# One 3 MB load in place of two for the first expert of each late pair, in a mixture-of-experts kernel

## What is computed

```python
routed = moe_dispatch(x, eidx, gates, lw['exp_w_gate'], lw['exp_w_up'], lw['exp_w_down'])
shared = swiglu(x, lw['sh_w_gate'], lw['sh_w_up'], lw['sh_w_down'])
# swiglu: (silu(x @ w_gate) * (x @ w_up)) @ w_down
```

## Time and profile before

| | us |
|---|---|
| median of 3 runs | 1326.27 |
| lowest and highest | 1323.79, 1328.75 |
| the profiled execution | 1324.62 |
| its span, first to last instruction | 1322.5 |
| TensorE busy in it | 1224.0 |
| ScalarE, VectorE busy | 239.2, 280.4 |

### The profile page before, as it was taken

One profiled execution on the slowest core, in us unless ns is written; L12 is line 12 of the kernel. 1 busy time (PEld: TensorE's weight loads), 2 busy tenths in 40 slices (PEclk: granted clock), 3 DMA queues, 4 the chain that ended last, 5 costly groups with the idle time before them and its releaser, 6 DMA issues.

```text
span 1322.5 us, 22616 instructions
## 1 busy us (share of the span) xinstructions
PE 1224.0 (93%) x9596; PEld 836.7 (63%) x9596; DVE 280.4 (21%) x720; ACT 239.2 (18%) x533; POOL 2.8 (0%) x13
## 2 busy tenths in 40 slices
PE   7999999998998898889989999999899898889896
PEld 4566687666766465556565658866667564557464
DVE  1252362110011010111034425511010110011012
ACT  2363131110010110011034521411010101010102
POOL 0000000000000000000000000000000000000000
PEclk9999999999999898889999999999999998899899
DMA  9879849999999999999956653999999999999993
GB/s 401 329 311 352 348 183 420 401 424 408 428 425 426 424 428 427 427 424 424 422 238 252 248 230 146 418 415 424 426 408 421 425 429 425 426 425 429 423 420 160
DMA packets 51796, 496.60 MB, mean 375 GB/s; under 512 B 8848, under 2 KB 9104, under 8 KB 10256
## 3 DMA queue, kind: packets, MB, share of 16 engines
q1 hardware_dynamic: 47664, 493.62, 89.8%
q10 hardware_dynamic: 4064, 2.00, 0.5%
HBM read 493.60 MB, written 2.00 MB: 375 GB/s over the span
## 4 chain that ended last, share of the span: by engine, by line
PE 54%; DMA 36%; SPq 3%; DVE 3%; issue 2%; ACT 1%; DVEq 0%; ACTq 0%
DMA gu<-in_exp_w_both 33%; PE PS L2214 17%; PE PS L1718 7%; PE PS L2050 4%; PE PS L2141 4%; PE PS L2250 4%; PE PS L2148 3%; PE PS L1660 2%; DMA xh<-in_exp_w_both 2%; PE PS L1628 1%; PE PS L2099 1%; DMA gu<-in_w_in_wide 1%; SPq L621 1%; PE PS L1841 1%; PE PS L1852 1%
## 5 line engine op out<-in xcount | busy, mean ns | idle before, releaser
L2214 PE MATMUL PS<-gu,arena 128*32 128x256 f32 (+1 forms) x2848 | 241.2, 422 | 58.6 <-DMA gu<-in_exp_w_both 58.6
L2214 PEld LDWEIGHTS PS<-gu,arena 128*32 128x32 f32 (+1 forms) x2848 | 133.3, 125 | 154.4 <-DMA gu<-in_exp_w_both 65.8
L2141 PE MATMUL PS<-arena 128*128 128x128 f32 x1408 | 176.3, 278 | 0.5 <-ACT arena L1050 0.5
L2141 PEld LDWEIGHTS PS<-arena 128*128 128x128 f32 x1408 | 164.0, 192 | 17.8 <-issue 16.7
L2214 PE MATMUL PS<-arena 128*64 128x256 f32 x704 | 160.2, 386 | 9.3 <-DMA gu<-in_exp_w_both 9.0
L2148 PE MATMUL PS<-arena 128*128 128x256 f32 x704 | 160.2, 380 | 1.4 <-ACT arena L1033 1.4
L2250 PE MATMUL PS<-dn,arena 128*32 128x512 f32 (+1 forms) x688 | 160.2, 596 | 0.0
L2250 PE MATMUL PS<-arena 128*64 128x512 f32 (+1 forms) x336 | 152.6, 597 | 3.0 <-DVE arena L1533 1.6
L2148 PEld LDWEIGHTS PS<-arena 128*128 128x128 f32 x704 | 130.2, 190 | 20.5 <-ACT arena L1033 3.2
L2214 PEld LDWEIGHTS PS<-arena 128*64 128x64 f32 x704 | 96.1, 139 | 67.5 <-issue 22.8
L1539 DVE TENSOR_TENSOR arena<-arena,PS 128x256 f32<-128x256 f32 x44 | 18.5, 421 | 552.7 <-ACT arena L1046 552.7
(11 more groups left out here) (264 smaller groups left out, 1023.3 us busy)
## 6 DMA issues: line engine op xcount, KB each, us to landing
gu<-in_exp_w_both SPq DMA_DIRECT2D x72, 2048.0 KB, 20.2
dn<-in_exp_w_down SPq DMA_DIRECT2D x86, 1024.0 KB, 25.7
arena<-in_exp_w_down SPq DMA_DIRECT2D x42, 1024.0 KB, 26.4
gu<-in_w_ada_pieces SPq DMA_DIRECT2D x20, 2048.0 KB, 9.1
arena<-in_exp_w_both SPq DMA_DIRECT2D x20, 2048.0 KB, 23.1
gu<-in_exp_w_both SPq DMA_DIRECT2D x34, 1024.0 KB, 19.4
xh<-in_exp_w_both SPq DMA_DIRECT2D x12, 2048.0 KB, 35.4
gu<-in_w_in_wide SPq DMA_DIRECT2D x8, 2048.0 KB, 14.4
```

The lines of the kernel that those rows point to most:

```text
L2141: ins = mmul(PS[:, 4, (c % 4) * P:(c % 4) * P + P], h_tok[:, g, c], onehot[b][:, g], start=(g == 0), stop=(g == 1))
L2214: ins = mmul(PS[w * h:w * h + w, 5, FF * half:FF * half + FF], xg[:, k, w * h:w * h + w], weights[half][:, k], start=(k == 0), stop=(k == ...
```

## The change

The three matrices of an expert are laid side by side per partition: one tensor `in_exp_w` with 24 KB a partition, 3 MB an expert. All expert loads read from it. A gate-and-up load now takes 16 KB of each 24 KB, a down 8 KB, a half 8 KB. In `arena`, `fifth` and `fifth_dn` become neighbours, `fifth_whole`. For m = 3 to 7 the pair's first expert comes as one load of 3 MB, issued where its down was issued, and the sixth's gate and up go ahead of it. It is counted in `pair_in`; `pair_dn_in` then counts only the sixth's down, whose target is adapted in `pair`. TensorE's loop begins one turn later, and turn 3 is written out.

```diff
-        fifth = carve(2 * NC_ * FF)
+        fifth_whole = carve(2 * NC_ * FF + 2 * D)
+        fifth = fifth_whole[:, 0:2 * NC_ * FF]
...
-        fifth_dn = carve(2 * D).rearrange("p (j n) -> p j n", j=2)
+        fifth_dn = fifth_whole[:, 2 * NC_ * FF:].rearrange("p (j n) -> p j n", j=2)
...
+            def expert(l, x):
+                return t["exp_w"][l, bass.ds(x, 1)].rearrange("e p n -> (e p) n")
+
             def gate_and_up(l, x):
-                return t["exp_w_both"][l, bass.ds(x, 1)].rearrange("e p n -> (e p) n")
+                return expert(l, x)[:, 0:2 * BLOCK]
...
             def down(l, x):
-                return t["exp_w_down"][l, bass.ds(x, 1)].rearrange("e (p j) n -> (e p) (j n)", j=2)
+                return expert(l, x)[:, 2 * BLOCK:]
...
+            def load_whole_fifth(l, x, told):
+
+                sp.dma_start(fifth_whole, expert(l, x)).then_inc(S[told], 16)
...
                     sp.wait_ge(S["up_done"], m * 2 + (r0 + 4))
-                    both(range(RING, RING + 2), xp, "pair_in", "pair_up_in")
-                    sp.wait_ge(S["down_done"], m * 2 + (r0 + 4))
-                    for j in range(2):
-                        load_dn(RING + j, l, xp[j], "pair_dn_in")
+                    if last:
+                        both(range(RING, RING + 2), xp, "pair_in", "pair_up_in")
+                        sp.wait_ge(S["down_done"], m * 2 + (r0 + 4))
+                        load_dn(RING, l, xp[0], "pair_dn_in")
+                    else:
+                        load(RING + 1, l, xp[1], "pair_in")
+                        sp.wait_ge(S["down_done"], m * 2 + (r0 + 4))
+                        load_whole_fifth(l, xp[0], "pair_in")
+                    load_dn(RING + 1, l, xp[1], "pair_dn_in")
...
-                def pair(m, early=None, last=False, between=None):
+                def pair(m, early=None, last=False, between=None, whole=False):
...
+                    if last:
+                        dns_in = (S["pair_dn_in"], pair_dns_in + (32 * TURNS - 16 * WHOLE))
+                    elif whole:
+                        dns_in = (S["pair_dn_in"], m * 16 + (16 * (DOWN_TURN + 3) + pair_dns_in))
+                    else:
+                        dns_in = (S["pair_dn_in"], m * 32 + (32 + pair_dns_in))
...
-                with pe.Fori(DOWN_TURN + 1, TURNS - 1) as m:
+                quad(DOWN_TURN + 1)
+                pair(DOWN_TURN + 1)
+                with pe.Fori(DOWN_TURN + 2, TURNS - 1) as m:
                     quad(m)
-                    pair(m)
+                    pair(m, whole=True)
```

More of the change, by code:

```diff
@@ L580, in over_loads @@
                     x = expert_in(sp, l, bass.ds(e, 1))
[L581 to L585, removed]
+                    w = t["exp_w"][l, bass.ds(x, 1)].rearrange("e p n -> (e p) n")
+                    sp.dma_start(gu[:, expert_slot[l][1], :], w[:, 0:2 * NC_ * FF]).then_inc(o["w"], 16)
+                    sp.dma_start(dn[:, 1].rearrange("p j n -> p (j n)"), w[:, 2 * NC_ * FF:]).then_inc(o["w"], 16)
                 sp.wait_ge(o["pe"], E * PE_STEPS * OW + BEFORE)
@@ L596, in _ @@
             BLOCK = NC_ * FF
+            def expert(l, x):
+                return t["exp_w"][l, bass.ds(x, 1)].rearrange("e p n -> (e p) n")
             def gate_and_up(l, x):
-                return t["exp_w_both"][l, bass.ds(x, 1)].rearrange("e p n -> (e p) n")
+                return expert(l, x)[:, 0:2 * BLOCK]
             def gate_or_up(l, x, half):
-                return t["exp_w_both"][l, bass.ds(x, 1), :, half * BLOCK:(half + 1) * BLOCK].rearrange("e p n -> (e p) n")
+                return expert(l, x)[:, half * BLOCK:(half + 1) * BLOCK]
             def down(l, x):
-                return t["exp_w_down"][l, bass.ds(x, 1)].rearrange("e (p j) n -> (e p) (j n)", j=2)
+                return expert(l, x)[:, 2 * BLOCK:]
             def place(j, l):
@@ L2266, in _ @@
                 pairs_in, pair_ups_in = l * 32 * TURNS, l * 32
+                WHOLE = TURNS - 3 - DOWN_TURN
+                pair_dns_in = l * (32 * TURNS - 16 * WHOLE)
                 def quad(m, early=None, last=False):
@@ L2274, in quad @@
                                  (S["quad_dn_in"], m * 64 + 64 * t0))
-                def pair(m, early=None, last=False, between=None):
+                def pair(m, early=None, last=False, between=None, whole=False):
                     second, second_dn = (halves(sixth), dn[:, RING - 1]) if early is None else (own[0], dn[:, 0])
                     ups = [(S["pair_up_in"], pair_ups_in + 32)] if last else []
+                    if last:
[4 more added lines that the diff above has]
+                        dns_in = (S["pair_dn_in"], m * 32 + (32 + pair_dns_in))
                     expert_round(m, 3, (halves(fifth), second), (fifth_dn, second_dn), [(S["pair_in"], m * 32 + (32 + pairs_in))],
-                                 ups, (S["pair_dn_in"], m * 32 + 32 * t0), last=last, between=between)
+                                 ups, dns_in, last=last, between=between)
                 for m in range(DOWN_TURN + 1):
@@ L2373, in laid_out @@
     named["w_ada_first"] = first_third.transpose(2, 0, 1, 3).reshape(NC_ // 2, D, 4 * P)
-    named["exp_w_both"] = np.concatenate([named.pop(n).reshape(DEPTH, E, P, NC_ * FF) for n in ("exp_w_gate", "exp_w_up")],
-                                         axis=-1)
+    named["exp_w"] = np.concatenate([named.pop(f"exp_w_{n}").reshape(DEPTH, E, P, NC_ * FF) for n in ("gate", "up", "down")],
+                                    axis=-1)
     uq = i["mla_w_uq"].reshape(DEPTH, Q_LORA, MLA_H, MLA_QK)
```

## The result

The changed kernel takes 1335.17 us (median of 4 runs, 1334.61 to 1338.0) against 1326.36 us: a ratio of 1.0069, 95% interval 1.0054 to 1.0083. The forecast was 1323.9 us. The profiled execution took 1334.69 us with a span of 1332.6, so 10.1 us more than the span before.

A forecast was written before the change was run, and what follows sets the result against it. The expert load stream at 426 GB/s was taken as the bound. Layer-end gains of 2.0 + 0.4 = 2.4 us took the profiled 1324.62 to 1322.2 us; the median's 1.65 us offset gave 1323.9, range 1319 to 1330.

The forecast's parts named there:

- part 6: TensorE's loop: turn 3 written out gives PE two more rounds as straight code; taken as 0 us.
- Part 1: Pair loads of turns 3 to 7: one load instead of two saves 0.09 us each, 0.9 us in all.
- Part 2: All expert loads: stepping 24 KB between partitions costs 0; bad end, 420 instead of 426 GB/s.
- Part 3: Load stream: the fifth's 2 MB issued 11.2 us later; the stream stays full and the next quad's loads land as before.
- Part 4: Loop pairs: start 1.9 us later in layer 0, 1.4 in layer 1, covered by the quad's wait; price 0.
- Part 5: Layer ends: layer 0's last quad all but loses its pause, gaining 2.0 us; layer 1 gains 0.4 us.
- the pair's wait lengthens the turns: Rival at the pair's first matmul: lateness above 5.1 us slows the turns, 1335 us if 6.0 us late; chance 0.02.
- the 24 KB stride slows the stream: Rival on expert loads: the stream falls to 420 GB/s, 13.5 us more, 1339 us; chance 0.07.
- gap between loads: Rival in the load stream: each load less returns a hidden fixed cost, say 1 us, giving 1316 us; chance 0.04.
- fixed 2 us per load: Rival's larger form in the load stream: ten loads less save 20 us, giving 1306 us.

The follow-up runs named there:

- e2: The kernel before with only turn 3 written out on TensorE, old layout and load order kept: 1336.59 us, ratio 1.0072.
- e1: The changed kernel with turn 3 put back in TensorE's loop instead of written out: 1323.03 us, ratio 0.9975.
- e4: The changed kernel with turn 3 in the loop and the fifth's late load split into 2 and 1 MB: 1326.32 us, ratio 0.9987.
- e3: The kernel before with only the joint layout, all expert loads strided at 24 KB a partition: 1324.63 us, ratio 0.9984.
- e5: The kernel before with 56 matmuls that never run added to each layer's skipped overflow branch: 1338.42 us, ratio 1.0096.

## Why the prediction was wrong

The step that failed is part 6: "PE gets two more rounds as straight code, turns 0 to 2 are so already. [...] I take 0; no row prices it." Its price was 10 us (e2: 1336.59 against 1326.82). The two rounds themselves do run as fast as in the loop: from its quad to the next, turn 3 takes 41.27 us written out (374.12 to 415.39) and 41.97 in the loop of e1 (371.87 to 413.84). What was missed is that they move the code behind them, and that there the kernel has a jump over the overflow branch followed at once by the last pair, which sets the end of the layer. The page of before had a row from which to ask, its 51 instruction fetches, and the source had the branch; neither was weighed, and no rival named it.

The sum of that term, from the trace after: in layer 1 the step from 3.3 to 10.1 us behind, which is 6.8. The chain has 3.46 us of it as idle after the data had landed (3.60 against 0.14 before), and 2.85 as gates at the lower clock (6.52 against 3.67). The rest, some 0.5, is data that landed later after the last quad's ups (15.6 against 15.1 us). In layer 0 the chain has 1.49 us of idle after the landing at 652.76.

The other steps, by e1, in which the failed one is undone:
- Part 1: right. 0.09 us per merge was taken; the loop's turns of e1 and e4 differ by 0.09.
- Part 2: right. 426 GB/s at the 24 KB stride (e3).
- Part 3: right. The stream stayed full (426 to 427 GB/s), and the late issue was free (e4).
- Part 4: right in its size. Counted back from the next quad's start, the pair starts 1.9 us later in layer 0 (22.06 us before it in e1, 23.93 in the kernel before) and 1.4 in layer 1 (22.08 in the changed kernel, 23.50 before), both as forecast. PE waits 2.1 us there, in layer 1 more than the lateness, since the quad ahead now takes 8.80 us for its 128 gate and up matmuls, where it took 9.64. The quad's own wait is 3.7 us, as forecast. The clock did not fall to the lower level in the pair: in layer 0 of the changed kernel its gates and ups took 7.13 to 7.15 us, as in turn 2 (7.13).
- Part 5: right for layer 0. The ups of the last quad start at 635.12 after a pause of 0.39 us and take 3.66 (forecast 634.8 and 3.66); the last pair starts at 650.10 (forecast 649.8). In layer 1 it stands 1.18 us for the sixth's half, which lands 15.9 us after the last quad's ups instead of the 15.1 before; that was not forecast.
- The sum: 2.4 us faster was forecast; e1 is 3.3 us faster by the ratio (0.25%, interval 0.11 to 0.40%). The layout alone (e3) is 2 us faster, which no step explains, and layout and late order together (e4) are 1.7 us faster, with an interval that reaches to nothing. So the size of the forecast is met, but how much of the 3.3 us is the merge's is not shown term by term.

Of the rivals, "the pair's wait lengthens the turns" and "the 24 KB stride slows the stream" would have given a time near the measured one, 1335 and 1339 us. e1, which has the pair's wait, and e3, which has the stride, show that neither did; the agreement was chance. No gap between loads came back as a gain, and the Trainium skill's fixed 2 us per load, a fit of loads issued by GpSimd where these are issued by SyncE, did not show: in the turns ten loads less gave about 0.9 us.

What stays open: why PE stands up to 4.5 us for one block of which the packet is 1.1 us, what fills up to 1.65 us before the packet and 1.3 to 1.8 us behind it, and what decides when the fetch starts. The packet itself is hardly slower than elsewhere: the instruction packets of the changed kernel between 689 and 832 us, where the load queues are less full, last 0.9 to 1.0 us. The time around it may still depend on the full stream of loads; no run took the loads away.

## What to carry to other kernels

Code that is written out, lengthened or shortened moves all code behind it on its engine. Look, in the page before, at the instruction queue and, in the source, for jumps over skipped blocks that are followed by work on the path that sets the end; add the fetch to the sum as a range, here from zero to 4.5 us each, and the slow clock behind it, here up to 2.9 us. When a profile shows idle with "issue" as its releaser, look for an instruction packet in that stretch, and test it with code that never runs. Here the loop could have kept its turn, since the old waits' targets and the new agree at turn 3.

## What the runs showed that was not expected

- 56 matmuls that never run cost the kernel 11.5 us (e5).
- An idle of 4.32 us, 3.60 of it after the data had landed, cost 2.85 us more through TensorE's clock, granted at 0.55 over the 6.4 us that followed. The length of a pause alone does not tell: 2.22 us in the kernel before were followed by a clock of 0.68 (in layer 0's last quad), 2.67 us in the changed one by the full clock (in layer 0's last pair).
- A row of 24 KB goes as one packet: the load queue has 46224 packets against 47664 before, 1440 fewer: 1280 packets of 24 KB stand for 2560 of 16 and 8 KB, and there are 160 fewer under 512 B, 16 for each of ten merges.
- The joint layout alone made the kernel 0.16% faster (interval 0.07 to 0.24%) with turns of the same length.
